# Gated stages of a hybrid model: the token's inverse root moved from the operand to the eviction, with the hand-over through a PSUM bank

## The chip, the cores and the metric

One core of one Trainium2 chip runs the whole program in one launch. The metric is the device time in microseconds, taken as the median of several runs. Everything is float32; each large product is made of three products of float32r halves.

## The reference, cut to what matters

A stack of two blocks on 256 tokens of width 1024. The first block has four layers (two RWKV-7 layers, a stick-breaking attention, a sparse attention), the second has two layers on two streams, `x` and `ctx`. Between the mixers stand eleven gated units (feed-forward), each fed by a root-mean-square norm; four take the plain norm, seven the modulated one:

```python
def rms_norm(x, g):
    xf = x.astype(jnp.float32)
    y = xf * lax.rsqrt(jnp.mean(xf * xf, axis=-1, keepdims=True) + RMS_EPS)
    return (y * g.astype(jnp.float32)).astype(x.dtype)

def swiglu(h, w_gu, w_down):
    g, u = jnp.split(h @ w_gu, 2, axis=-1)
    return (jax.nn.silu(g) * u) @ w_down
...
        x = x + swiglu(rms_norm(x, norm_ffn[i]), ffn_w_gu[i], ffn_w_down[i])
...
        x = x + 0.5 * mx[2] * swiglu_2(modulated_norm(x, norm_g[l, 0], mx[0], mx[1]), *ffn1)
```

`modulated_norm` is the same norm with a gain per channel and a shift per channel added after it. Width inside a unit: 2816.

## The kernel before, in words

Activations lie transposed in SBUF: 128 partitions hold channels, the free axis holds 8 chunks of 256 tokens (`X`, `CTX`). A projection is a list of weight panels, each 128x1024 (8 chunks deep, 128 output columns), planned in one fixed order (`order`). For each panel SyncE loads `raw` (4 slots), ScalarE makes the rounded half `whi` (L571), GpSimd the rest `wlo = raw - whi` (L561), and TensorE runs 24 matmuls (8 chunks by three products, L658), each of 256 columns, into one of four PSUM banks. ScalarE makes the `whi` of panel p+4 when panel p is done (semaphore `panels_done`), so it runs four panels ahead. VectorE empties the banks (`bank_free`).

A projection of 1024 outputs and depth 1024 has 8 steps of one panel. The down projection has 8 steps of three panels (8, 8 and 6 chunks). The up projection of a gated unit has 22 steps of two panels, gate and up; the two projections together have 1584 matmuls.

A gated unit (`act_ffn`, `pe_ffn`, `dve_ffn`) begins with the norm. ScalarE squares the 8 chunks into `W[8]` (L609; all but the last while the projection before still runs), TensorE sums them over partitions with a matrix of ones in 8 float32 matmuls (L738, each two records), ScalarE takes the square root (L724), VectorE the reciprocal `RSTD` (L744), then for each chunk VectorE multiplies by gain and `RSTD` (L760), ScalarE makes the rounded half `AH` (L731 with a shift, L733 without), VectorE the rest `AL` (L753 or L755). TensorE starts on a chunk when its `AL` is there. In the up loop ScalarE takes `silu` of the gate bank (L789), VectorE multiplies it with the up bank into bank 5 (L807) and splits the product into `HH` and `HL` (L809, L811).

Between the last gated unit of the first block (`ffn3`) and the first of the second (`f10x`) the context rows are turned (TensorE L1820, VectorE L1839) and `dve_ada` makes shifts and gains (L1911, L1915, L1921) and a scalar `LAM` (L1924, TensorE L1902, ScalarE L1898). `dve_ada` runs again between `f20x` and `f11x`. The eleven units follow these projections: four a mixer's output projection of the first block (`ffn0` to `ffn3`), three a mixer's output projection of the second (`f20c`, `f20x`, `f21x`), four a down projection (`f10x`, `f10c`, `f11x`, `f11c`).

## Time and profile before

| | |
|---|---|
| time, median of 3 runs | 4366.14 us (4362.85 to 4371.75) |
| profiled execution | 4345.92 us, span 4344.1 us |
| TensorE busy | 3865.0 us, 89% of the span |
| GpSimd busy | 2664.3 us, 61% |
| ScalarE busy | 1936.8 us, 45% |
| VectorE busy | 1603.7 us, 37% |
| granted TensorE clock, mean | 0.947 of full speed |

The profile is of one execution. Busy shares are averages over all stages: TensorE is the engine that most stages wait for, and what matters for a change is the stretch in which it waits.

### The profile page before, as it was taken

The page shows a single profiled execution, that of the slowest core. Times are in us where ns is not written, and L with a number is a line of the kernel's source. Part 1 is how long each engine was busy: PE and PEld are TensorE (multiplying, and loading weights), DVE is VectorE, ACT ScalarE, POOL GpSimd, SP SyncE. Part 2 cuts the span into 40 slices and gives each one's busy share as a digit, 9 for nine tenths or more (in the row PEclk, how much of TensorE's full clock was granted, in tenths as well). Part 3 has the DMA queues.
Part 4 walks back from the last instruction along what each step waited for, and adds up shares of the span by engine and source line. Part 5 has one row for each costly group of instructions (what it writes and reads, how often), then busy time and mean ns, then how long its engine had stood idle before and what let it go on. Part 6 is the DMA issues. An engine that isn't in the chain of part 4 may idle for free.

```text
span 4344.1 us, 94128 instructions
## 1 busy us (share of the span) xinstructions
PE 3865.0 (89%) x36305; PEld 3657.7 (84%) x36305; DVE 1603.7 (37%) x3002; ACT 1936.8 (45%) x2635; POOL 2664.3 (61%) x1186
## 2 busy tenths in 40 slices
PE   5897998999798989799999978998889999997799
PEld 5676997998498857798999868997789899996798
DVE  4544214214621454312121473227531212148421
ACT  3213446543353322444454464535544445446453
POOL 4103873786177400587877747875578687874676
PEclk8998999999799999899999999999899999999899
DMA  5453652564157445465665525654356565653455
GB/s 153 150 196 103 184 171 77 174 189 120 31 174 194 136 142 180 124 193 169 194 174 166 163 81 163 192 164 117 112 160 193 155 184 172 174 148 93 134 170 150
DMA packets 1177130, 664.74 MB, mean 153 GB/s; under 512 B 30141, under 2 KB 1138441, under 8 KB 1176743
## 3 DMA queue, kind: packets, MB, share of 16 engines
q1 hardware_dynamic: 1176871, 661.06, 51.7%
q8 instruction: 190, 3.11, 0.3%
q14 instruction: 69, 0.57, 0.0%
HBM read 659.92 MB, written 1.05 MB: 152 GB/s over the span
## 4 chain that ended last, share of the span: by engine, by line
PE 69%; issue 14%; POOL 7%; DVE 6%; ACT 2%; SPq 1%; DMA 1%; POOLq 0%; DVEq 0%; ACTq 0%
PE bank L658 56%; POOL wlo L561 7%; PE bank L738 2%; PE bank L637 2%; PE bank L991 1%; PE bank L821 1%; PE bank L1062 1%; PE bank L1085 1%; DVE RSTD L744 1%; PE bank L1091 1%; DVE W L760 1%; PE bank L894 1%; PE bank L1068 1%; PE bank L1093 1%; DVE AL L716 0%
## 5 line engine op out<-in xcount | busy, mean ns | idle before, releaser
L561 POOL TENSOR_TENSOR wlo<-raw,whi 128x1024 fp32r<-128x1024 f32 (+3 forms) x1182 | 2664.1, 2270 | 1656.0 <-ACT whi L571 1646.5
L658 PE MATMUL bank<-AH,whi 128*128 128x256 f32 x6320 | 1802.0, 285 | 192.0 <-DVE AL L716 104.5
L658 PE MATMUL bank<-AL,whi 128*128 128x256 f32 x6320 | 1784.1, 282 | 0.0
L658 PE MATMUL bank<-AH,wlo 128*128 128x256 f32 x6320 | 1782.1, 282 | 0.0
L571 ACT ACTIVATE whi<-raw 128x1024 fp32r<-128x1024 f32 (+3 forms) x1182 | 1173.2, 995 | 1159.0 <-PE bank L658 1006.2
L658 PEld LDWEIGHTS bank<-AH,whi 128*128 128x128 f32 x6320 | 1220.7, 193 | 209.9 <-issue 180.8
L658 PEld LDWEIGHTS bank<-AH,wlo 128*128 128x128 f32 x6320 | 1223.1, 194 | 0.0
L658 PEld LDWEIGHTS bank<-AL,whi 128*128 128x128 f32 x6320 | 1222.6, 193 | 0.1
L658 PE MATMUL bank<-HH,whi 128*128 128x256 f32 x1936 | 536.1, 277 | 0.0
L658 PE MATMUL bank<-HL,whi 128*128 128x256 f32 x1936 | 536.1, 277 | 0.0
L658 PE MATMUL bank<-HH,wlo 128*128 128x256 f32 x1936 | 536.1, 277 | 0.0
L807 DVE TENSOR_TENSOR bank<-silu,bank 128x256 f32<-128x256 f32 x242 | 103.9, 429 | 952.7 <-PE bank L658 952.7
L658 PEld LDWEIGHTS bank<-HH,wlo 128*128 128x128 f32 x1936 | 364.9, 188 | 0.0
L658 PEld LDWEIGHTS bank<-HL,whi 128*128 128x128 f32 x1936 | 363.4, 188 | 0.0
L658 PEld LDWEIGHTS bank<-HH,whi 128*128 128x128 f32 x1936 | 363.4, 188 | 0.0
L789 ACT ACT_TABLE_LOAD x101 | 129.6, 1283 | 175.0 <-PE bank L658 175.0
L789 ACT ACTIVATE silu<-bank 128x256 f32<-128x256 f32 x242 | 93.1, 385 | 248.4 <-PE bank L658 247.3
L704 DVE TENSOR_TENSOR X<-X,bank 128x256 f32 x64 | 27.0, 422 | 310.2 <-PE bank L658 310.2
L706 DVE SCALAR_TENSOR_TENSOR X<-bank,mod_x,X 128x256 f32 x48 | 23.2, 484 | 265.8 <-PE bank L658 265.8
L809 DVE CAST HH<-bank 128x256 f32 x242 | 102.9, 425 | 36.5 <-DVE bank L807 17.1
L658 PE MATMUL bank<-BRH,whi 128*128 128x256 f32 x240 | 77.6, 323 | 42.7 <-DVE BRL L716 18.2
L811 DVE TENSOR_TENSOR HL<-bank,HH 128x256 f32 x242 | 102.8, 425 | 31.3 <-DVE HH L809 2.9
(336 smaller groups left out, 4144.1 us busy)
## 6 DMA issues: line engine op xcount, KB each, us to landing
raw<-in_ffn_w SPq DMA_DIRECT2D x420, 512.0 KB, 3.8
raw<-in_w_in SPq DMA_DIRECT2D x182, 512.0 KB, 3.8
raw<-in_ffn_w_gu SPq DMA_DIRECT2D x176, 512.0 KB, 3.8
ada_raw<-in_w_ada SPq DMA_DIRECT2D x96, 512.0 KB, 6.0
raw<-in_ffn_w_down SPq DMA_DIRECT2D x64, 512.0 KB, 4.2
raw<-in_rw_w_rkv SPq DMA_DIRECT2D x48, 512.0 KB, 4.3
raw<-in_w_ada SPq DMA_DIRECT2D x48, 512.0 KB, 5.1
raw<-in_ffn_w SPq DMA_DIRECT2D x56, 384.0 KB, 3.5
```

The source lines that it names most:

```text
L561: pool.tensor_tensor(wlo[slot][:, 0:n], raw[slot][:, 0:n], whi[slot][:, 0:n], ALU.subtract).then_inc(lo_ready, 1)
L571: act.activation(whi[slot][:, 0:n], raw[slot][:, 0:n], ACT.Copy).then_inc(hi_ready, 1)
L637: mm = pe.matmul(ps, o, w, start=k == c == n == 0, stop=k == g.pps - 1 and c == nk - 1 and n == 2)
L658: mm = pe.matmul(ps[:, 0:o.shape[2]], w, o[:, k0 + c, :], start=tile not in started and c == n == 0, stop=last_panel and c == nk - 1 and n ...
L738: mm = pe.matmul(bank[4][:, 0:S], ones[:, :], W[8][:, c * S:(c + 1) * S], start=c == 0, stop=c == C - 1)
L744: dve.reciprocal(RSTD[:, :], STD[:, :]).then_inc(dve_step, 1)
L760: op = dve.scalar_tensor_tensor(h[:, o], x[:, o], gain(c), RSTD[:, :], ALU.mult, ALU.mult)
L789: act.activation(silu[j % 2][:, :], ps[:, 0:S], ACT.Silu).then_inc(silu_ready, 1)
L807: dve.tensor_tensor(hidden, silu[j % 2][:, :], banks[1][:, 0:S], ALU.mult).then_inc(bank_free, 2)
L809: dve.tensor_copy(HH[:, o], hidden).then_inc(dve_step, 1)
L811: dve.tensor_tensor(HL[:, o], hidden, HH[:, o], ALU.subtract).then_inc(hidden_ready, 1)
L821: mm = pe.matmul(bank[first + c // 2][:, (c % 2) * S:(c % 2 + 1) * S], mat, src[:, c * S:(c + 1) * S], start=True, stop=True)
```

## The change

The operand of a gated unit no longer carries the token's inverse root. ScalarE multiplies each finished chunk of the residual by the gain alone, into bank 5 (`SCALED`), squares the chunk into the other half of that bank (`SQUARE`), and makes `AH` by the same product; VectorE makes `AL` from the bank and adds the squares up. All this runs chunk by chunk inside the projection before (`SPLIT_AFTER`). TensorE sums two tiles of squares (`SQSUM`, `SQLAST`) after its first panel, and VectorE multiplies gate and up by `RSTD` when it empties the banks. Where the norm has a shift, the operand gets two more columns per chunk (the shift's rounded half and its rest), the matmuls on `AH` run over 258 columns, and the two extra columns of the result, summed, are the shift's share, added as a bias. So `AH` has a chunk every 320 columns, and the vector table `VEC` lies in the last 62 of them. The operands of the output projections go to `OUTH`, `OUTL` (`W[7]`, `W[8]`), since `A` is being filled for the unit behind.

```diff
+        AW = S + 64
-        AH, AL = sb("AH", C * S, F32R), sb("AL", C * S, F32R)
+        AH, AL = sb("AH", C * AW, F32R), sb("AL", C * S, F32R)
+        VEC = sb("VEC", C * AW, at=a_at)
...
+        A_SHIFTED = (AH_v[:, :, 0:S + 2], AL_v)
+        OUT = (v3(OUTH), v3(OUTL))
...
+        SPLIT_AFTER = {"rw0.out": "ffn0", "sb.out": "ffn1", "ds.out": "ffn2", "rw3.out": "ffn3", "ffn3.down": "f10x",
+                       "f10x.down": "f10c", "mix0c.o": "f20c", "mix0x.o": "f20x", "f20x.down": "f11x",
+                       "f11x.down": "f11c", "mix1x.o": "f21x"}
...
+                if split_for:
+                    if s > 0:
+                        act.wait_ge(bank_free, g.t0 + s)
+                    act_high_parts(act, split_for, chunks_until(FFN[split_for].after_own, s))
...
+        def act_high_parts(act, name, until):
+            f = FFN[name]
+            for c in range(high_made[0], until):
+                xc = f.x[:, c * S:(c + 1) * S]
+                if c == C - 1:
+                    act.wait_ge(partial_squares, after(act, partial_squares))
+                elif c:
+                    act.wait_ge(scaled_taken, after(act, scaled_taken))
+                act.activation(SCALED, xc, ACT.Copy, scale=f.gain(c))
+                if c < C - 1:
+                    act.activation(SQUARE, xc, ACT.Square)
+                act.activation(AH_v[:, c, 0:S], xc, ACT.Copy, scale=f.gain(c)).then_inc(hi_part, 1)
+                if c == C - 1:
+                    act.activation(SQLAST[:, :], xc, ACT.Square).then_inc(last_square, 1)
+            high_made[0] = max(high_made[0], until)
+
+        def dve_low_parts(dve, name, until):
+            for c in range(low_made[0], until):
+                dve.wait_ge(hi_part, after(dve, hi_part))
+                dve.tensor_tensor(AL_v[:, c, :], SCALED, AH_v[:, c, 0:S], ALU.subtract).then_inc(operand_ready, 1)
+                if c == 0:
+                    dve.tensor_copy(SQSUM[:, :], SQUARE).then_inc(scaled_taken, 1)
+                elif c < C - 1:
+                    done = scaled_taken if c < C - 2 else partial_squares
+                    dve.wait_ge(scaled_taken, after(dve, scaled_taken))
+                    dve.tensor_tensor(SQSUM[:, :], SQUARE, SQSUM[:, :], ALU.add).then_inc(done, 1)
...
         def act_ffn(act, name, x, shift=None):
-            act_norm(act, x, W[7], shift)
...
+                if k == 0 and isinstance(s, int) and s == 0:
+                    act.wait_ge(sums_ready, after(act, sums_ready))
+                    act.activation(STD[:, :], bank[4][:, 0:S], ACT.Sqrt, bias=eps[:, 0:1], scale=1.0 / D).then_inc(std_ready, 1)
+                if k == 1:
+                    act.wait_ge(gate_ready, after(act, gate_ready))
...
+                dve.tensor_tensor(bank[6][:, b * S:(b + 1) * S], banks[0][:, 0:S], RSTD[:, :], ALU.mult).then_inc(gate_ready, 1)
+                dve.wait_ge(panels_done, after(dve, panels_done))
+                if f.shift is not None:
+                    dve.tensor_reduce(offset[:, 2:3], banks[1][:, S:S + 2], AX_X, ALU.add)
+                dve.tensor_tensor(up, banks[1][:, 0:S], RSTD[:, :], ALU.mult).then_inc(bank_free, 2)
...
+        def dve_ffn_turning(dve, name, l, turn=None):
+            dve_ffn(dve, name)
+            dve_modulation(dve, l)
+            dve_lambda_in(dve, l)
+            between = {3: lambda: dve_lambda_out(dve, l)}
+            if turn:
+                between |= {0: lambda: turn(0), 1: lambda: turn(1)}
+            dve_residual(dve, f"{name}.down", FFN[name].x, FFN[name].out_gate, between)
```

`chunks_until` gives chunk s-1 at step s where the unit reads the stream that the projection is just updating (nine units), and chunk s where it reads the other stream (`f10c`, `f11c`). `dve_ffn_turning` serves `ffn3` and `f20x`: the context's turning and the making of shifts and gains move from behind the down projection into it.

On ScalarE, the end of the first RWKV layer's output projection and the head of `ffn0`, before (`W_92` is the squares' tile):

```order
L571 ACTIVATE whi_56<-raw_52 128x1024
L609 ACTIVATE W_92<-X 128x256 x2
L724 ACT_TABLE_LOAD
L724 ACTIVATE STD<-bank,eps 128x256
L733 ACTIVATE AH<-W_91 128x256 x8
L789 ACT_TABLE_LOAD
L789 ACTIVATE silu_81<-bank 128x256
```

and of the change at the same place:

```order
L583 ACTIVATE whi_56<-raw_52 128x1024
L642 ACTIVATE bank<-X,VEC 128x256
L644 ACTIVATE bank<-X 128x256
L645 ACTIVATE AH<-X,VEC 128x256
L642 ACTIVATE bank<-X,VEC 128x256
L645 ACTIVATE AH<-X,VEC 128x256
L647 ACTIVATE sq_98<-X 128x256
L583 ACTIVATE whi_53<-raw_49 128x1024
L886 ACT_TABLE_LOAD
L886 ACTIVATE STD<-bank,eps 128x256
L583 ACTIVATE whi_54<-raw_50 128x1024
L891 ACT_TABLE_LOAD
```

The square root and its table load now stand behind the first panel of the up projection, and what is left of the last two chunks stands ahead of it.

On VectorE, the stretch between `ffn3` and `f10x` before:

```order
L704 TENSOR_TENSOR X<-X,bank 128x256
L101 REGISTER_ALU
L101 COMPARE_AND_BRANCH
L1839 COPY CTX<-bank 128x512 x4
L1911 TENSOR_TENSOR mod_x<-both_115,VEC 128x72
L1915 SCALAR_TENSOR_TENSOR gain_x<-mod_x,VEC 128x8 x3
L1921 TENSOR_SCALAR mod_x<-mod_x 128x8 x2
L1911 TENSOR_TENSOR mod_c<-both_115,VEC 128x72
L1915 SCALAR_TENSOR_TENSOR gain_c<-mod_c,VEC 128x8 x3
L1921 TENSOR_SCALAR mod_c<-mod_c 128x8 x2
L1924 TENSOR_TENSOR LAM<-VEC_76 128x2
```

and with the change, where they stand behind the up loop of `ffn3` and ahead of its first residual:

```order
L2057 TENSOR_TENSOR mods<-both_119,VEC 128x72
L2061 SCALAR_TENSOR_TENSOR gains<-mods,VEC 128x8 x3
L2067 TENSOR_SCALAR mods<-mods 128x8 x2
L2057 TENSOR_TENSOR mods<-both_119,VEC 128x72
L2061 SCALAR_TENSOR_TENSOR gains<-mods,VEC 128x8 x3
L2067 TENSOR_SCALAR mods<-mods 128x8 x2
L2040 TENSOR_TENSOR LAM<-VEC_76 128x2
L791 TENSOR_TENSOR X<-X,bank 128x256
L669 CAST AH<-mods 128x8
L671 TENSOR_TENSOR AH<-mods,AH 128x8
L1971 COPY CTX<-bank 128x512 x2
L791 TENSOR_TENSOR X<-X,bank 128x256
```

Thirteen small operations, all from SBUF to SBUF, moved from a stretch between two projections to one in which panels are being prepared.

## Rows read from the trace of the kernel before

**Rows 1.** The page, part 1: busy time, share, instructions.

```profile
PE 3865.0 (89%) x36305; PEld 3657.7 (84%) x36305; DVE 1603.7 (37%) x3002; ACT 1936.8 (45%) x2635; POOL 2664.3 (61%) x1186
```

**Rows 2.** Waits of TensorE: total us, times, longest us.

```profile
PE bank L658 <- DVE AL L716: 104.5, 9, 18.8
PE bank L658 <- DVE AL L753: 49.1, 11, 5.6
...
PE bank L658 <- DVE AL L755: 25.3, 6, 4.5
```

**Rows 3.** The chain that ended last, whole span: start us, us, what.

```profile
774.59 3.47 PE bank L738 x16
782.21 181.68 PE bank L658 x1584
...
3396.89 189.74 PE bank L658 x1581
3586.62 3.47 PE bank L738 x16
3595.63 182.85 PE bank L658 x1584
```

**Rows 4.** The same chain, from 770 to 784 us.

```profile
778.09 0.48 ACT STD L724
...
778.66 1.76 DVE RSTD L744
```

**Rows 5.** The same chain, from 1968 to 1996 us.

```profile
1975.91 0.03 issue
...
1976.53 0.67 PE bank L1820 x4
...
1983.21 0.35 PE bank L1902 x2
...
1993.73 2.38 PE bank L658 x8
```

**Rows 6.** Windows of 4 us: busy by engine, then clock, DMA share, GB/s.

```profile
778.00:782.00 4.00, 0.05 (x1) 0.00 (x0) 3.30 (x6) 1.51 (x4) 0.12 (x1) 1.00 0.62 184
782.00:786.00 4.00, 3.79 (x17) 3.61 (x18) 4.00 (x13) 2.26 (x6) 0.00 (x0) 0.57 0.00 0
786.00:790.00 4.00, 4.00 (x37) 4.00 (x37) 0.39 (x2) 2.77 (x4) 0.11 (x1) 1.00 0.01 4
...
2888.00:2892.00 4.00, 2.19 (x19) 1.98 (x17) 0.42 (x1) 2.12 (x2) 2.09 (x1) 1.00 1.16 294
...
2388.00:2392.00 4.00, 2.49 (x12) 2.52 (x13) 0.09 (x1) 2.62 (x3) 4.00 (x3) 0.71 1.02 253
```

**Rows 7.** Windows of 100 us, line L658 alone: PE, PEld, clock, DMA.

```profile
440.00:540.00 100.00, 100.00 (x852) 100.00 (x851) 1.00 0.64 184
800.00:900.00 100.00, 100.00 (x885) 100.00 (x884) 1.00 0.66 192
```

**Rows 8.** Groups of instructions, shapes apart: busy us, mean ns, idle before.

```profile
L571 ACT ACTIVATE whi<-raw 128x1024 fp32r<-128x1024 f32 x998 | 1056.3, 1059 | 1011.1 <-PE bank L658 859.1 <-PE bank L637 53.6 <-DMA raw<-in_w_in 49.5
...
L789 ACT ACT_TABLE_LOAD x101 | 129.6, 1283 | 175.0 <-PE bank L658 175.0
...
L2323 DVE TENSOR_TENSOR W<-W,hid 128x256 f32 x48 | 42.9, 894 | 7.3 <-DVE hid L2321 3.7
...
L2321 DVE TENSOR_TENSOR hid<-silu,bank 128x256 f32<-128x256 f32 x72 | 30.4, 422 | 120.4 <-ACT silu L2207 116.0 <-DVE BRL L716 1.2 <-DVE W L2323 0.6
...
L731 ACT ACTIVATE AH<-W,mod_x 128x256 fp32r<-128x256 f32 x48 | 23.1, 505 | 22.9 <-DVE W L760 22.9
```

**Rows 9.** Timeline of GpSimd: an output projection, then an up projection.

```profile
758.81 2.40 POOL L561 TENSOR_TENSOR wlo<-raw,whi 128x1024 fp32r<-128x1024 f32 x1 [0.31 <-ACT whi L571]
...
844.29 9.50 POOL L561 TENSOR_TENSOR wlo<-raw,whi 128x1024 fp32r<-128x1024 f32 x4 [1.39 <-ACT whi L571]
```

**Rows 10.** Timeline of VectorE between `f20x` and `f11x`.

```profile
3381.71 2.62 DVE L1915 SCALAR_TENSOR_TENSOR gain_x<-mod_x,VEC 128x8 f32<-128x8 f32 x3
```

More of the change, by code:

```diff
@@ L270, in build @@
         HL = sb("HL", FC * S, F32R, at=w_at[0] + FC * S * 4)
+        OUTH = sb("OUTH", C * S, F32R, at=w_at[7])
+        OUTL = sb("OUTL", C * S, F32R, at=w_at[8])
+        SQSUM, SQLAST = (sb(f"sq{k}", S, at=w_at[5] + (C // 2 + k) * S * 4) for k in range(2))
         VF = sb("VF", C * S)
@@ L601, in act_panels, with chunks_until @@
                 per |= work.per
-            steps_of(act, g, per, step, last_straight=True)
+            if then:
+                per |= then.per
+            steps_of(act, g, per, step, peel=then is not None, last_straight=True)
         squared = [0]
+        high_made, low_made = [0], [0]
+        SCALED, SQUARE = bank[5][:, 0:S], bank[5][:, S:2 * S]
+        def chunks_until(own, s):
+            return s if own or s == 0 else s + 1
+        def act_high_parts(act, name, until):
[13 more added lines that the diff above has]
+            high_made[0] = max(high_made[0], until)
@@ new lines, in dve_shift_columns, with dve_residual @@
+        def dve_shift_columns(dve, name):
+            f = FFN[name]
+            if f.shift is None:
+                return
+            m = f.shift.unsqueeze(2)
+            dve.tensor_copy(AH_v[:, :, S:S + 1], m).then_inc(dve_step, 1)
+            dve.wait_ge(dve_step, after(dve, dve_step))
+            dve.tensor_tensor(AH_v[:, :, S + 1:S + 2], m, AH_v[:, :, S:S + 1], ALU.subtract)
+        def dve_residual(dve, name, x, gate=None, between=None):
+            g = G[name]
+            split_for = SPLIT_AFTER.get(name)
+            if not split_for:
+                dve_tiles(dve, name, take_residual(dve, x, gate))
+                return
+            tile = dve_tiles(dve, name, take_residual(dve, x, gate), by_hand=True)
+            own = FFN[split_for].after_own
+            for s in range(g.steps):
+                tile(s)
+                if s == 0:
+                    dve_shift_columns(dve, split_for)
+                dve_low_parts(dve, split_for, chunks_until(own, s))
+                if between and s in between:
+                    between[s]()
+            dve.wait_ge(bank_free, tiles_of(name))
@@ new lines, in pe_ffn, with norm_sums, pe_ffn_down @@
+        def pe_ffn(pe, name):
+            def norm_sums():
+                for k, (t, made) in enumerate(((SQSUM, partial_squares), (SQLAST, last_square))):
+                    pe.wait_ge(made, after(pe, made))
+                    mm = pe.matmul(bank[4][:, 0:S], ones[:, :], t[:, :], start=k == 0, stop=k == 1)
+                mm.then_inc(sums_ready, 1)
+            pe_panels(pe, f"{name}.up", chunked=True, after_first=norm_sums)
+        def pe_ffn_down(pe, name, by_hand=False):
+            return pe_panels(pe, f"{name}.down", chunked=True, chunk_ready=hidden_ready, by_hand=by_hand)
@@ L847, in build @@
         L_, VT, BT, CT = (W[7][:, k * Q4:(k + 1) * Q4] for k in range(4))
-        work = [sb(f"scan{k}", Q4, at=a_at + k * Q4 * 4) for k in range(7)]
+        work = [sb(f"scan{k}", Q4, at=l_at + k * Q4 * 4) for k in range(7)]
         IY, IX, IT, LOFF, RHS, SOL, STATE = (t[:, :] for t in work)
@@ L2464, in pe_second @@
         def pe_second(pe):
[L2465 to L2471 removed]
+            pe_ffn_all(pe, "f10x")
+            pe_ffn_all(pe, "f10c")
             pe_mix(pe, 0, "c")
[L2473 removed]
+            pe_ffn_all(pe, "f20c")
             pe_mix(pe, 0, "x")
[L2475 to L2478 removed]
+            pe_ffn_turning(pe, "f20x")
+            pe_ffn_all(pe, "f11x")
+            pe_ffn_all(pe, "f11c")
             pe_mix(pe, 1, "c")
             pe_mix(pe, 1, "x")
[L2481 removed]
+            pe_ffn_all(pe, "f21x")
             pe_norm(pe)
@@ L2517, in _ @@
                     sp_lora(sp, 1)
-                if g.name == "f10x.up":
+                if g.name == "ffn3.down":
                     sp_ctx(sp)
```

331 lines of the change are left out of this document (195 added, 136 removed).

## The prediction, made before the changed kernel ran

> **What bounds the kernel now.** I read the page first: TensorE is busy 3865 of 4344 us [rows 1], so a gain must come from its 479 idle us or from work taken off it. The list of its waits says where they are. Two entries belong to the norms whose multiplied chunks it waits for, 49.1 and 25.3 us [rows 2]; they include norms ahead of mixers, which stay. The largest, 104.5 us, is the split ahead of output projections and of the RWKV projections; it stays too. A wait alone does not price a norm, though, since TensorE sums squares in it. So I went to the chain. The sums of `ffn1` start at 774.59 and the up projection at 782.21, 7.6 us later; for `f11c` it is 9.0 [rows 3]. In between lie the eight sums (3.47), the root (0.48), the reciprocal (1.76) and the first multiplied chunks [rows 3, 4]. Nine of the eleven units have such a gap, between those two values, 71.9 us in sum. `f10x` also waits for the context's turning and for `dve_ada`: 1975.91 to 1993.73, 17.8 us [rows 5]. For `f11x` it is 15.2 us from the second kind of operation of `dve_ada`, at 3381.71, to the up projection at 3396.89 [rows 3, 10], and ahead of it lie the last residual and `dve_ada`'s first operation, which I put at 1.6: 16.8.
>
> A second cost lies behind the gap. In `ffn1`'s gap TensorE does nothing from 778 to 782; the clock is at 0.57 in the next 4 us and full again after (half is 1.2 GHz, full 2.4) [rows 6]. In a full window of an up loop 885 matmuls overlap 100 us, 882.5 without those that only hang over its left edge, so one takes 113.3 ns [rows 7]; 1584 of them make 179.5 us, and the chain has 181.7 for `ffn1` and 182.9 for `f11c` [rows 3]. So 2.2 to 3.4 us a unit go to the slow clock and to chunks that come slower than TensorE takes them, 31 us for eleven. What the change can touch is 71.9 + 17.8 + 16.8 + 31 = 138 us.
>
> **The same stream has two rates.** In `ffn0` 852 matmuls fall into 100 us, 117.7 ns each, at the same full clock [rows 7]. Two of the eleven units run so in this execution. Nothing waits in either, and I do not know what picks the rate. One unit at the slow rate costs 1584 x 4.4 ns = 7 us.
>
> **The change, part by part.**
>
> *At the restart, nine units.* Count from T, the end of the projection's last matmul. ScalarE owes one panel's `whi` (1.06 us), then chunk 6: a scaled copy, a square, `AH`. `AH` with a scalar from a table takes 0.505 [rows 8]; I take 0.5, 0.4 and 0.5, less what overlaps, 1.2 us: T+2.25. VectorE, with the residual behind it, makes `AL` and adds the square, 0.42 each, the price of its multiplication by a bank [rows 8]: T+3.1. Only then may ScalarE write chunk 7 into the bank, two operations, 0.9: T+4.05. `AL` is there at T+4.6. TensorE starts chunk 0 at T and would want chunk 7 after 21 matmuls, at T+2.2. Stall: 2.4 us. The two sums behind the first panel are a quarter of the eight, 0.87. Together 3.3, times nine: 29.7 us.
>
> *The other two* (`f10c`, `f11c`) have chunk 6 ready; chunk 7 follows at T+2.5, stall 0.3, with the sums 1.2 each: 2.4 us.
>
> *Turning and scalar.* TensorE keeps its 16 transposes, four of which take 0.67, and two `LAM` products, 0.35 each time [rows 5]: 3.4 us.
>
> *Clock.* A stall of 2.4 us, in two pieces around a chunk, is shorter than the 8 us that cost the clock. Short stalls go both ways: TensorE was busy 2.19 of 4 us around 2890 and the clock stayed at 1.00, 2.49 of 4 us around 2390 and it was 0.71 [rows 6]. I take one in three of the nine to cost what half the clock costs in 3.4 us, 1.7: 5 us. Bounds: 0 and 15.
>
> [...]
>
> *Root, reciprocal, table loads* leave the path: the first up eviction ends some 10.5 us after T (first panel with its stall 5.0, `whi` 1.06, load 1.28, root 0.48, reciprocal 1.76, two multiplications [rows 4, 8]). TensorE needs those banks back for the third step, 14.2 us after T (four panels of 2.72, stall and sums). The cover is about 4 us. Each us beyond it costs 1 us in each of eleven units.
>
> *The up loop.* VectorE goes from three operations a step to five of 0.42 and, with a shift, two tiny ones: 2.6 us of a 5.4 us step. ScalarE's work per step is the same. Neither gets near TensorE. In an output projection ScalarE now has 1.06 + 1.2 of 2.72 us a panel. Cover if wrong: four slots, of which the panel itself needs 1.06 + 2.4 us.
>
> *GpSimd* is the engine with no room: 2.40 us a panel in an output projection, four in 9.50 of 10.9 us in an up loop [rows 9]. Does more work on VectorE slow it or get slowed by it? VectorE's multiplication of SBUF by a bank takes 422 ns, and its sum of two SBUF tiles of the same shape, in the same loop, 894 on average [rows 8]. Three operations of 8 columns took 2.62 us together while a panel was made [rows 10]. So two SBUF operands wait for GpSimd to finish and one bank operand does not. All new operations of the loop and of `AL` read a bank. They cost what they cost alone.
>
> The Trainium skill has this as a rule: the two engines share a port pair that is locked for a whole instruction, when VectorE reads two SBUF tensors or copies in its two-port mode (SBUF — State Buffer, "SBUF: two separate sides"). The trace agrees, 894 against 422.
>
> *Thirteen small SBUF operations* move into that traffic, at the end of `ffn3` and `f20x`, and two more (the shift's columns) with each shift. Each may wait up to 2.40 us: 31 us if each meets a panel, some 3 us if none. After a panel GpSimd is idle 0.3 us, room for one or two; I take 15 us from T+4. The first residual of the down projection, due 7.5 us after its start, then comes at 19. ScalarE waits for that residual at step 1, from 16 on; TensorE has four panels in hand. In `f20x` that is covered. In `ffn3` TensorE itself waits behind step 1 (at 15.9) for VectorE's copies of the first half of the context, which come at 20 to 23: 4 to 7 us. With 31 us instead, ScalarE would be held, panels would stop, GpSimd fall idle and VectorE be free, so the loss ends near 10 a unit. I take 6 for both; bounds 0 and 20.
>
> *258 columns.* 7 units x 22 steps x 2 panels x 8 chunks x 2 products = 4928 matmuls have two more columns. No row shows that width. From below: a matmul takes 113.3 ns where 256 columns at 2.4 GHz need 106.7, so something else paces it and two columns may be free. From above within the stream: 2/2.4 = 0.83 ns each, 4 us. Far end: a second pass of the stream, 107 ns each. I take 1 us, as the row at 113.3 leaves 6.6 ns.
>
> [...]
>
> *At nothing:* chunks 320 apart (the split's copies keep rows of 256 adjacent columns), `OUTH`/`OUTL`, the moved scan tiles, the tables. The split into the strided `AH` stands on the path ahead of the RWKV projections; if it went at half its pace it would cost about 1.2 us six times, 7.
>
> **Sum.** After: 29.7 + 2.4 + 3.4 + 5 + 6 + 1 = 47.5 us against 138. Saved 90.5. The profiled execution, 4345.92 (its span and 1.8 around it), would be 4255. The median of the runs is 20 us above that execution; two slow-rate units of eleven in the profile leave room for more of them in the runs. I carry the difference over: 4366 - 91 = 4275.
>
> **The rivals.**
>
> 1. *As above*: nearly all gaps go. 4275, own range 4250 to 4295. Chance 0.65.
> 2. *A new wait takes over part.* The late chunk 7, VectorE's blocked operations or the thin cover of the first eviction cost 3 to 8 us more in most units. For: the last two chunks go through one bank and back and forth twice. Against: each step is priced from a row. 4300 to 4345; 0.15, of which 0.03 lies within 0.2% of no change and 0.01 above.
> 3. *The rate.* With fewer restarts whole runs of units share one rate. If nine more units ran at 117.7 it would be 63 us back: 4338; half of it 4307. For: the rate holds through both projections of a unit. Against: most restarts in the profile chose 113.3. Chance 0.10. The opposite, fewer slow ones than the timed runs had and no clock loss, gives 4230 to 4245: 0.06.
> 4. *Slower: the 258 columns fall off the fast path.* Place: the `AH` products of the seven shifted units. It decides from 90.5 us / 4928 = 18 ns each; with a second pass of 107 it is 527 - 91 = 436 more, 4802. For: no row has this width. Against: all that the trace shows is proportional to columns. Chance 0.04.
>
> **How the numbers follow.** Faster by over 0.2% (9 us, about what can be told from no change): 0.65 + 0.11 + 0.10 + 0.06 = 0.92. Same 0.03. Slower 0.01 + 0.04 = 0.05. The range takes all of case 1, half of each neighbour below and above it and most of the lower part of case 2: 4245 to 4312.
>
> **What would show it.** The sums should be two matmuls behind the first panel; the distance between the last matmul of a projection and the first of the unit should be under 0.5 us, and chunk 7 should come 4.6 us after T. `AL` from a bank should take 0.42. TensorE's wait in `ffn3`'s down projection should be 4 to 7 us. Matmuls on `AH` in `f10x` should keep 885 in 100 us. I am wrong if the first eviction comes later than 14 us after the unit began, if GpSimd's panel grows beyond 2.5 us in the up loop, or if 100 us of a shifted unit hold fewer than 850.

## The result, and the profile after

The changed kernel takes 4289.61 us (median of 4 runs, 4284.73 to 4293.22) beside 4364.50 for the kernel before on the same chip (4 runs, 4353.61 to 4371.75): a ratio of 0.983, 95% interval 0.9806 to 0.9854. That is 75 us faster. The forecast was 4275, its range 4245 to 4312.

The page of the changed kernel, part 1, has 132 matmuls fewer, and TensorE busy for 14 us less, not more [rows 1]:

```profile
PE 3850.9 (90%) x36173; PEld 3647.9 (85%) x36173; DVE 1846.4 (43%) x3797; ACT 1865.4 (43%) x2633; POOL 2673.1 (62%) x1186
```

The waits of TensorE (total us, times, longest us). L804 is now the split ahead of output and RWKV projections, L841 and L843 the low parts of the norms that stayed, L654 the new low part out of the bank:

```profile
PE bank L743 <- DVE OUTL L804: 73.6, 7, 18.8
PE bank L743 <- DVE AL L804: 30.2, 2, 15.3
...
PE bank L743 <- DVE AL L841: 18.2, 4, 5.6
...
PE bank L743 <- DVE AL L654: 16.7, 18, 1.3
...
PE bank L743 <- DVE AL L843: 8.3, 2, 4.2
```

The two norm entries of [rows 2], 49.1 and 25.3 us, have become 18.2 and 8.3 (the norms that stayed) and 16.7 (new). Now one restart, `ffn1`, as the chain of the work that ended last shows it (start us, us, what). The projection ends at T = 767.64:

```profile
763.89 3.75 PE bank L743 x33
767.64 0.02 issue
767.66 0.28 ACT whi L583
767.95 0.69 issue
768.63 0.46 ACT bank L642
769.09 0.31 ACT bank L644
769.40 0.44 ACT AH L645
769.84 0.02 issue
769.86 0.42 DVE AL L654
770.29 0.34 DVE sq L660
...
770.72 0.10 ACT bank L642
...
771.13 0.50 ACT AH L645
...
771.72 0.44 DVE AL L654
772.16 0.04 issue
772.20 0.86 PE bank L743 x3
773.06 1.71 PE bank L903 x4
```

TensorE starts the unit at once, but it gets its chunk 7 only 4.56 us after T: chunk 6 is made first, behind a cast of a weight panel, and chunk 7 waits for the square at 770.29. The two float32 sums of squares (L903, four records) follow behind the three products of chunk 7, here at a low clock (0.57 granted between 772 and 776). The gap of 7.6 us [rows 3] has become a stall of some 2 us inside the stream.

Then the stream itself. Windows of 100 us, line L743 alone: us, then TensorE and its weight loads with their counts, clock, DMA share, GB/s. The first is `ffn0`, the second `ffn1`, the third `ffn3`, the last three `f10x`, `f10c` and `f11x`:

```profile
440.00:540.00 100.00, 100.00 (x851) 100.00 (x850) 1.00 0.64 186
800.00:900.00 100.00, 100.00 (x885) 100.00 (x884) 1.00 0.65 190
1800.00:1900.00 100.00, 100.00 (x884) 100.00 (x884) 1.00 0.69 203
2000.00:2100.00 100.00, 100.00 (x845) 100.00 (x844) 1.00 0.62 182
2190.00:2290.00 100.00, 100.00 (x847) 100.00 (x846) 1.00 0.62 181
3380.00:3480.00 100.00, 100.00 (x844) 100.00 (x843) 1.00 0.63 184
```

In every unit with a shift some 40 matmuls are missing from 100 us, at full clock and with no wait. Taking off the 2.5 that only hang over an edge, as before, one matmul takes 118.7 ns there in place of 113.3 [rows 7] (the mean distance from start to start, read from the trace, is 118.9). It isn't the wide ones alone: the distances from start to start between 2000 and 2090 us are, on the mean, 118.0 behind the first 258-column product, 120.4 behind the 256-column one on `AL`, 118.3 behind the second wide one.

Lengths of the seven up projections with a shift, first matmul to first matmul of the down projection, in us, read from the traces (`e1_narrow` and `e10`, the kernel with a steady run of wide products, are experiments below):

```
               f10x   f10c   f20c   f20x   f11x   f11c   f21x    sum
before        122.1  122.7  123.1  122.1  128.1  122.8  123.5  864.4
changed       130.3  126.6  128.8  128.8  128.8  126.6  128.8  898.7
e1_narrow     124.7  125.4  123.0  127.6  124.7  125.4  123.0  873.8
e10           126.4  126.4  126.4  126.4  126.4  126.4  126.4  884.8
```

All stretches together, profile against profile: ahead of the units 95.8 us less, up projections 40.7 more, down projections 2.4 more, 52.7 us in sum (spans 4344.1 and 4291.4).

### The profile page after: what moved, and what is told of

Read it like the earlier page. It is cut to its first block, busy times and chain, and to the rows that moved or that the text cites. A ratio compares the mean times of both kernels' runs of the same rounds, so it can differ in the third digit from the quotient of the medians.

```text
span 4291.4 us, 94696 instructions
## 1 busy us (share of the span) xinstructions
PE 3850.9 (90%) x36173; PEld 3647.9 (85%) x36173; DVE 1846.4 (43%) x3797; ACT 1865.4 (43%) x2633; POOL 2673.1 (62%) x1186
## 4 chain that ended last, share of the span: by engine, by line
PE 68%; issue 15%; POOL 8%; DVE 6%; ACT 2%; SPq 1%; DMA 1%; POOLq 0%; DVEq 0%; ACTq 0%
PE bank L743 56%; POOL wlo L573 8%; PE bank L722 2%; PE bank L1123 1%; PE bank L1194 1%; PE bank L953 1%; PE bank L1217 1%; PE bank L1223 1%; PE bank L826 1%; PE bank L1026 1%; PE bank L1200 1%; PE bank L1225 1%; DVE W L848 0%; DVE RSTD L832 0%; DMA raw<-in_rw_w_rkv 0%
## 5 line engine op out<-in xcount | busy, mean ns | idle before, releaser
L743 PE MATMUL bank<-AH,whi 128*128 128x256 f32 (+1 forms) x5872 | 1665.7, 284 | 85.4 <-DVE AL L804 30.2
L743 PE MATMUL bank<-AL,whi 128*128 128x256 f32 x5872 | 1659.8, 283 | 0.0
L743 PE MATMUL bank<-AH,wlo 128*128 128x256 f32 (+1 forms) x5872 | 1654.3, 282 | 0.0
L743 PEld LDWEIGHTS bank<-AH,whi 128*128 128x128 f32 x5872 | 1128.1, 192 | 98.7 <-issue 51.6
L743 PEld LDWEIGHTS bank<-AL,whi 128*128 128x128 f32 x5872 | 1121.7, 191 | 0.6
L743 PEld LDWEIGHTS bank<-AH,wlo 128*128 128x128 f32 x5872 | 1121.7, 191 | 0.0
L743 PE MATMUL bank<-HH,whi 128*128 128x256 f32 x1936 | 536.4, 277 | 0.0
L743 PE MATMUL bank<-HH,wlo 128*128 128x256 f32 x1936 | 536.0, 277 | 0.0
L743 PE MATMUL bank<-HL,whi 128*128 128x256 f32 x1936 | 536.0, 277 | 0.0
L743 PEld LDWEIGHTS bank<-HH,whi 128*128 128x128 f32 x1936 | 364.6, 188 | 0.0
L743 PEld LDWEIGHTS bank<-HH,wlo 128*128 128x128 f32 x1936 | 363.6, 188 | 0.0
L743 PEld LDWEIGHTS bank<-HL,whi 128*128 128x128 f32 x1936 | 363.4, 188 | 0.0
L743 PE MATMUL bank<-OUTH,whi 128*128 128x256 f32 x448 | 132.0, 295 | 73.6 <-DVE OUTL L804 73.6
L932 DVE TENSOR_TENSOR bank<-bank,RSTD 128x256 f32<-128x256 f32 x242 | 103.2, 426 | 159.6 <-PE bank L743 159.5
L743 PEld LDWEIGHTS bank<-OUTH,whi 128*128 128x128 f32 x448 | 91.3, 204 | 75.7 <-issue 75.7
L743 PE MATMUL bank<-OUTL,whi 128*128 128x256 f32 x448 | 130.5, 291 | 0.0
L743 PE MATMUL bank<-OUTH,wlo 128*128 128x256 f32 x448 | 130.3, 291 | 0.0
```

The source lines that it names most:

```text
L743: mm = pe.matmul(ps[:, 0:o.shape[2]], w, o[:, k0 + c, :], start=tile not in started and c == n == 0, stop=last_panel and c == nk - 1 and n ...
L932: dve.tensor_tensor(up, banks[1][:, 0:S], RSTD[:, :], ALU.mult).then_inc(bank_free, 2)
```

## The experiments

The kernel before was timed again beside each set of runs: 4369.81 us beside `e1` to `e4`, 4360.23 beside `e5` to `e8`, 4355.78 beside `e9` to `e12`, 4364.50 beside the changed kernel. Kernels of different sets are therefore compared by their ratio to it (in brackets) and by their traces, and a few us between their medians show nothing.

**The width.** The seven shifted units get narrow operands; nothing is left to reduce, so the two reduces of a step become memsets, and the shift is left out.

```diff
-        A_SHIFTED = (AH_v[:, :, 0:S + 2], AL_v)
+        A_SHIFTED = (AH_v[:, :, 0:S], AL_v)
-                    dve.tensor_reduce(offset[:, b:b + 1], banks[0][:, S:S + 2], AX_X, ALU.add)
+                    dve.memset(offset[:, b:b + 1], 0.0)
```

> The products of the seven shifted units are 256 columns wide again, and the two reduces of each step are replaced by memsets of the offset to nought; so this kernel leaves out the modulation's shift, and all else is the changed kernel. Theory A, the width: the two extra columns cost 5.7 ns on each of 7392 matmuls (mean start to start 119 ns against 113.3 in the units without a shift), so the seven up projections return to 113.3 ns, some 885 matmuls in 100 us in place of 845, and the time falls by 7392 x 5.7 ns = 42 us, from 4289.6 to about 4248. Theory B, the layout or the traffic: the operand's chunks 320 columns apart, or ScalarE and VectorE at the banks, slow these matmuls; then they stay at 119 ns and the time stays within 5 us of 4289.6.

Measured: 4273.75 us (ratio 0.98, 0.9766 to 0.9833), by the medians 16 us under the changed kernel and not 42. Windows in `f10x` and in `f10c`:

```profile
1990.00:2090.00 100.00, 100.00 (x885) 100.00 (x884) 1.00 0.65 192
...
2160.00:2260.00 100.00, 100.00 (x852) 100.00 (x851) 1.00 0.63 184
```

Four of the seven units run at 113.3 ns, three (`f10c`, `f20x`, `f11c`) at 117.7, and these three keep 117.8 through their down projections, 2.4 us more each. The theory named the right cause and the wrong price: narrow units take part in the choice between two rates that `ffn0` already showed before the change [rows 7]; the wide ones never get the quick one. The up projections of these seven are 24.9 us shorter, the down projections of the three 7 us longer; 18 net, against 16 of the medians. The reduces went with the width here, but they aren't the cause: in the last two kernels with wide products below, 16 short runs of 258-column products that nobody reduces went at 118.0 to 120.4 ns on the mean.

**One wide product of three.**

```diff
+                            o = o[:, k0 + c, 0:S if w is wl else o.shape[2]]
-                            mm = pe.matmul(ps[:, 0:o.shape[2]], w, o[:, k0 + c, :], start=...
+                            mm = pe.matmul(ps[:, 0:o.shape[1]], w, o, start=...
```

> Of the three products of a chunk only the first (high weights by high operand) is 258 columns wide; the product of the low weights is 256 wide, so the kernel leaves out the low weights' part of the shift. Reduces and layout are the changed kernel's. If each wide matmul carries its own cost (8.5 ns, two in three wide now), the mean falls from 119 to about 116.2 ns and the time by 21 us to about 4269. If it is enough for the rate that wide and narrow matmuls alternate, it stays at 119 ns and 4290. If the reduces or the layout were the cause, it stays there too.

Measured: 4290.51 us (0.9839, 0.9801 to 0.9877). A window in `f10c`:

```profile
2160.00:2260.00 100.00, 100.00 (x852) 100.00 (x851) 1.00 0.63 184
```

That is exactly the slow rate, 117.7, in all seven units; so there is no price per wide product: one in three is enough to hold the slow rate, and the second adds 1.0 ns on the mean. It came with something not expected: the down projections behind all seven units began at 117.8, and six of them kept it (62.2 us in place of 59.8; that of `f20x` went to 113 behind the float32 product for `LAM`), where the changed kernel has 113.3 seven times.

**More columns, off and on a coarser grid.** First 264 columns with chunks 328 apart, then 272 with chunks 336 apart.

```diff
-        AW = S + 64
+        AW = S + 72          # second kernel: S + 80
-        A_SHIFTED = (AH_v[:, :, 0:S + 2], AL_v)
+        A_SHIFTED = (AH_v[:, :, 0:264], AL_v)          # second: 0:272
```

> The two high-operand products are 264 columns wide in place of 258 (chunks 328 columns apart; the six columns more hold copies of the shift and are not read behind). If a column past 256 costs what the two extra ones seem to cost (8.5 ns a wide matmul, 4.3 ns a column), a wide matmul takes 34 ns more than a narrow one, the mean is about 136 ns and the time about 4290 + 7392 x 17 ns = 4415. If there is one step at 256 and columns cost what they cost elsewhere (113.3 ns for 256, 0.44 ns each), six columns cost 2.7 ns on two in three matmuls, 13 us: about 4303.

> The two high-operand products are 272 columns wide and the operand's chunks 336 columns apart: both are multiples of 64 bytes, as 264 columns and chunks 328 apart were not (those put every product that reads the operand, narrow ones too, at a mean of 119.4 ns). Theory A, the grid: what lies on such a grid runs at the quick rate and the columns cost 0.44 ns each, so the shifted units come to 113.3 + 2/3 x 16 x 0.44 = 118.0 ns a matmul, those without a shift back to 113.3 or 117.8, and the time to about 4280. Theory B, any difference of widths between neighbours holds a stretch at the slow rate: 117.8 + 4.7 or more, 122.5 to 124 ns, and a time of about 4315 to 4325.

Measured: 4331.32 us (0.9914, 0.9888 to 0.994) and 4342.38 us (0.9963, 0.9947 to 0.998). Windows of 264 columns, in `ffn0` (256-column products, chunks 328 apart) and in `f10c`:

```profile
450.00:550.00 100.00, 100.00 (x843) 100.00 (x842) 1.00 0.63 184
...
2200.00:2300.00 100.00, 100.00 (x828) 100.00 (x828) 1.00 0.61 179
```

and of 272 columns, in `ffn1` (256-column products, chunks 336 apart) and in `f10c`:

```profile
800.00:900.00 100.00, 100.00 (x852) 100.00 (x851) 1.00 0.63 185
...
2200.00:2300.00 100.00, 100.00 (x819) 100.00 (x819) 1.00 0.61 179
```

Columns beyond 258 are cheap: 118.7, 121.1 and 122.5 ns for 258, 264 and 272, 0.27 to 0.4 ns of the mean for each column more. So it is a step between 256 and 258, theory B of the second kernel. (No kernel here has all three products wide, so whether the width or the change of width from one product to the next holds the slow rate isn't separated.) Both times lie above what the step and the columns give, since a second cost came in: with chunks 328 or 336 apart no up projection ran at 113.3, not even with 256 columns (119.0 and 117.7 ns; the distances rise at the first matmul on `AH`, ahead of any wait), while the down projections, whose chunks are 256 apart, began at 113.3 eleven times of eleven in both. With chunks 256 or 320 apart both rates occur. 1024 and 1280 bytes are multiples of 256 bytes, 1312 and 1344 are not; two strides on each side are few for a rule, but my rule in the expectation, 64 bytes, falls with 1344.

**Can single wide products set the rate?**

```diff
+                if marked and not first_step and n == S and (o is A[0] or o is OUT[0] or o is HID[0]):
+                    t = AH if o is A[0] else OUTH if o is OUT[0] else HH
+                    at = c * (AW if o is A[0] else S)
+                    return ps[:, 0:S + 2], w, t[:, at:at + S + 2]
```

> The runs so far show two rates of 256-column matmuls, 113.3 and 117.8 ns, and that a stretch keeps its rate: behind a unit whose last product is 258 (or 264) columns wide, the projection down ran at 113.3 in 18 of 18 cases; behind one whose last product is narrow it kept 117.8. In this kernel the first and one late product of each step of every projection without a shift are 258 columns wide too (the two more columns are not read). Theory A: a wide product brings a slow stretch back to the quick rate within a few matmuls, so nearly all stretches without a shift show a median of 113 ns (of 256-column ones at full clock less than 10% slow, against 47% in the changed kernel), and the time falls by 5 to 20 us, to about 4278, the more the more of a run was slow. Theory B: a wide product among quick ones as often throws them onto the slow rate; then most of these stretches show 118 and the time rises by 20 to 60 us.

Measured: 4318.59 us (0.9903, 0.9875 to 0.9932), by the medians 29 us more than the changed kernel: theory B. Behind their start three of the four up projections without a shift run at 117.5 ns on the mean and `ffn0` at 115.3. Most down projections take 61.1 us, between the 59.8 of the quick and the 62.2 of the slow rate: stretches of 113 and of 118 take turns in them. A single wide product among narrow ones turns the rate both ways.

**The scan's tiles in their new place, all else as before.**

```diff
-        work = [sb(f"scan{k}", Q4, at=a_at + k * Q4 * 4) for k in range(7)]
+        work = [sb(f"scan{k}", Q4, at=l_at + k * Q4 * 4) for k in range(7)]
```

> The kernel before with one part of the change alone: the scan's scratch tiles lie where the low-rank weights were, not in the operand's place. The changed kernel's two RWKV mixers came out some 8 to 10 us longer than the nine gaps' sum allows. If the place of these tiles costs that, the two stretches ahead of ffn0 and ffn3 (421.3 and 402.7 us before) are 4 us longer each and the time is some 8 us above the kernel before, 4374. If it is only chance in when the clock falls during the chain of the scan, the median stays within 5 us of the kernel before, and these two stretches scatter about 421 and 403.

Measured: 4354.81 us beside 4360.23 (0.9991, 0.9967 to 1.0014): no cost. The stretches ahead of `ffn0` and `ffn3` took 425.0 and 406.0 us, 3.7 and 3.3 more than in the first profile, and a second profile of the changed kernel had 415.4 and 397.3 where the first had 416.8 and 403.2. These stretches scatter by 4 to 6 us from one execution to the next; the gain that seemed to be missing there is within that.

**The hand-over through SBUF in place of the bank.**

```diff
-        SCALED, SQUARE = bank[5][:, 0:S], bank[5][:, S:2 * S]
+        SCALED, SQUARE = (sb(n, S, at=w_at[5] + (C // 2 + 2 + k) * S * 4)[:, :] ...
```

> The changed kernel with SCALED and SQUARE in SBUF in place of the bank, so that VectorE's subtraction for the low part and its sum of squares have both operands in SBUF. Theory A: such an operation can't run beside GpSimd's subtraction of a panel (2.40 us), as four of the moved modulation operations showed in ffn3 (2.35 us for one of some 0.05); at each restart the low part of chunk 6 or its square then waits for the end of GpSimd's panel, chunk 7 comes 1 to 2.4 us later, TensorE's waits on the low parts grow from 16.7 us to 26 to 38, the clock falls at more restarts, and the time rises by 12 to 35 us, to about 4310. Theory B: the bank matters little, since the chain is ScalarE's; then the waits stay within 3 us and the time within 5 us of 4290.

Measured: 4350.24 us (0.9967, 0.9942 to 0.9993), by the medians 61 us more than the changed kernel: theory A, and dearer than its upper end. The low part, one line of the trace (duration min/median/max), and TensorE's wait for it:

```profile
L654 DVE TENSOR_TENSOR AL<-scaled,AH x88: 424/1520/2496, 405.8 to 4146.6; 128x256 fp32r<-128x256 f32 x88
...
PE bank L743 <- DVE AL L654: 54.6, 27, 3.4
```

The same operation out of the bank, in the changed kernel:

```profile
L654 DVE TENSOR_TENSOR AL<-bank,AH x88: 416/425/426, 402.9 to 4089.9; 128x256 fp32r<-128x256 f32 x88
```

The waits explain 38 of the 61 us. Behind them the clock is low: the sums of nine of the eleven units ran at half the clock (1.35 us from the first to the next panel in place of 0.67), in the changed kernel those of three; at some 1.6 us a unit (`ffn1` took 124.7 us, `ffn3` 123.0, both at 113.3 ns) the six more make about 10 us. The bank is no detail of the change: without it four fifths of the gain are gone.

**The modulation twice.**

```diff
             dve_modulation(dve, l)
+            if l == 0:
+                dve_modulation(dve, l)
```

> The modulation of the first layer is computed twice in ffn3 (the second time gives the same numbers): 12 operations more on VectorE, 8.3 us by the trace of the changed kernel, ahead of VectorE's first tile of the projection down. Theory A: what hides the modulation is the 9.3 us until TensorE asks for the transposed half of CTX (it waited 0.25 us there, from 1917.8), so the cover is used up and all of the addition shows: TensorE waits 8 to 9 us at the second group of transposes, and the time rises by 8 to 12 us (the clock falls behind such a wait), to about 4300. Theory B, four banks deep: VectorE may be a tile or two late at no price, the wait stays under 2 us and the time within 3 us of 4290.

Measured: 4309.34 us (0.9889, 0.9857 to 0.9921), 12.5 above the control below. TensorE's waits for the context's first half, first in the changed kernel, then here:

```profile
PE bank L1952 <- DVE CTX L1971: 0.2, 1, 0.2
```

```profile
PE bank L1952 <- DVE CTX L1971: 6.5, 1, 6.5
```

Theory A: the down projection of `ffn3` grew by 6.6 us in the profile. The wait was forecast at 8 to 9 us; of the 8.6 us that VectorE spends more, 2.1 came back at the cast L669, which took 0.17 us here and had waited for a panel in the changed kernel (2.30). The change put the modulation into a place that hides all of it but a quarter of a us, and nothing is left to spare there.

**A shorter restart.** The high parts of a chunk are made in the step of its own tile, the last chunk's ahead of the next cast and through bank 7, without the wait for the squares.

```diff
-            return s if own or s == 0 else s + 1
+            return s + 1 if own or s else 0
...
+                    if early and k == g.pps - 1:
+                        act.wait_ge(bank_free, g.t0 + s + 1)
+                        act_high_parts(act, split_for, C)
...
-                if c == C - 1:
-                    act.wait_ge(partial_squares, after(act, partial_squares))
-                elif c:
+                if c and c < C - 1:
                     act.wait_ge(scaled_taken, after(act, scaled_taken))
-                act.activation(SCALED, xc, ...
+                act.activation(SCALED if c < C - 1 else SCALED_LAST, xc, ...
```

> The high parts of a chunk are made in the same step as its tile, the last chunk's ahead of ScalarE's next cast and through a bank of its own, without the wait for the partial sum of squares. If the 2.4 us that TensorE waits for the last chunk at nine restarts is this chain (one chunk's work queued behind another's and the cast), chunk 7 is there before TensorE asks, the waits on the low parts fall from 16.7 us to under 3, the slow clock behind some restarts goes too, and the time falls by 17 to 27 us, to about 4268. Rival: the cast made 1.1 us later starves GpSimd's subtraction, whose panel takes 2.4 us, and TensorE waits for panels 2 or 3 later; then what is gained at chunk 7 is given back, and the time stays within 6 us of 4290.

Measured: 4279.73 us (0.9795, 0.9766 to 0.9823), by the medians 10 us less than the changed kernel, where 17 to 27 were forecast. The restart of `ffn1` (timeline of ScalarE and VectorE; the projection ends at 772.4):

```profile
773.04 0.48 ACT L644 ACTIVATE bank<-X,VEC 128x256 f32<-128x256 f32 x1 [1.21 <-DVE X L793]
773.46 0.49 ACT L647 ACTIVATE AH<-X,VEC 128x256 fp32r<-128x256 f32 x1
...
773.98 0.42 DVE L656 TENSOR_TENSOR AL<-bank,AH 128x256 fp32r<-128x256 f32 x1 [1.04 <-ACT AH L647]
774.16 1.04 ACT L583 ACTIVATE whi<-raw 128x1024 fp32r<-128x1024 f32 x1
```

Chunk 7 is there 2.0 us after the end, TensorE waits for no low part at all (16.7 us before), and no later wait took its place. The mechanism is as expected, and the shifted units show its price, since their rate is the same in both kernels: the seven take 884.9 us in place of 898.6, 2.4 us less in a unit like `f20c`, 13.7 in sum. The time fell by less than forecast because the units without a shift gave their part back to the slow rate: `ffn0`, `ffn1` and `ffn3` went up at 117.8 here, the first two down as well (in the changed kernel `ffn0` alone), so the four up projections are 3.9 us shorter in sum.

**A steady run of wide products.** On top of the shorter restart, wide products in the last step of the first block's output projections and plain up projections.

```diff
+                if burst and isinstance(s, int) and s == g.steps - 1 and k == g.pps - 1 and cc < nk - 1 and n != 1:
+                    t, at = (AH, c * AW) if o is A[0] else (OUTH, c * S)
+                    return ps[:, 0:S + 2], w, t[:, at:at + S + 2]
```

> The kernel with the shorter restart (no wait on the last chunk, 4279.7 us) and one thing more: in the last step of the four mixers' output projections of the first half and of the four up projections without a shift, the high-operand products of seven chunks are 258 columns wide, with a narrow chunk behind them. Theory A: a steady run of alternating widths always ends in the quick rate when narrow ones follow (18 of 18 so far, where single wide products among narrow ones only tipped it to and fro); then ffn0 to ffn3 up and ffn0 to ffn2 down run at 113.3 ns, where the shorter restart alone had 117.8 in five of these seven, and the time falls by 10 to 20 us to about 4265. Theory B: the rate behind such a run is as open as elsewhere; then it stays at 4280 within 6 us, with some of these stretches at 117.8.

Measured: 4268.81 us (0.9797, 0.9763 to 0.9832; 28 us under the control below, in the same set of runs), the lowest median here. But the shorter restart alone had 0.9795 in its set, so no gain over it is shown: the fall of 11 us between the two medians is no more than that of the kernel before, 14, between the two sets. The traces say why. The first half of theory A holds, a steady run leaves the quick rate, and the three down projections run at 113.3; but all four up projections run at 117.8, `ffn2` too, which had the quick rate in the shorter restart. All up and down projections together take 2045.2 us, in the shorter restart 2045.8. The distances from matmul to matmul (ns) in `ffn1`, at the end of the run of wide products and the beginning of the unit (first line), and around the sums of squares one panel later (second):

```
119 120 115 118 122 119 113 113 114 113 113 114 113 113 114
113 114 113 113 117 | sums, four records: 215 215 215 28 | 305 118 117 119 117 118 118 118
```

The run of wide products does end in 113. The two float32 products with the matrix of ones end it. At full clock, between narrow products and with no stall ahead of them that happened in 11 of 11 cases (four here, four in the next kernel, three in the shorter restart), and the one unit that came to the sums at 118 (`ffn2` in the shorter restart) left them at 113. The sums turn one rate into the other. Where a stall stands just ahead of them, either rate followed: in the changed kernel, at full clock, 118 in `ffn0` and 113 in `ffn3`. Other float32 products turn the rate too: the first eight transposes of the context in `ffn3`'s down projection did it in all nine traces whose projection came to them at 113 (the changed kernel's two included), and in the changed kernel the rest of that projection stayed at 118: 2 us of the 4.5 by which it is longer than before.

**One wide product, put last.**

```diff
+                        products = (...) if oh.shape[2] == S else ((wh, oh), (wh, ol), (wl, oh[:, :, 0:S]))
+                        if oh.shape[2] > S and k0 + c > 0:
+                            products = products[::-1]
```

> The kernel of the run before it, and in the shifted units only the product of the high weights by the high operand 258 columns wide, put last of the three (first in a tile's first chunk); the low weights' part of the shift is left out. With one wide product first of three, these units ran at 118.8 ns against 119.9, and the projections down behind them at 117.8 in place of 113.3. Theory A: the order decides only what comes behind: these units keep some 118.8 (8 us less than with two wide) and, ending wide, hand on the quick rate, so the time is some 8 us below that of the run before it, about 4258. Theory B: the last tile's rate doesn't depend on which product ended it; then the seven projections down run at 117.8 (2.4 us each) and the time is 8 us above it.

Measured: 4274.82 us (0.9816, 0.978 to 0.9853), 6 above the kernel of the run before it. The ranges of the two overlap; the traces decide for theory B: the shifted units shrank from 126.4 to 125.5 us, the seven down projections went from 59.8 to 62.2. What hands on the quick rate is not that a wide product comes last but the run with two of them around a narrow one: it did so behind every shifted unit of the six kernels that have it with 258 columns and no single wide ones, 42 of 42.

**The changed kernel again.**

> The changed kernel as it is, for a second profile of it on the chip of these runs. If the two RWKV stretches are chance, ahead of ffn0 and ffn3 scatter by some us about 417 and 403 us; the time should be 4290 within 5 us, the seven shifted units at 119.8 ns again and the projections down behind them at 113.3, as these follow from the layout and not from chance; ffn0's rate may be either.

Measured: 4296.79 us (4290.22 to 4303.99; 0.9859, 0.9824 to 0.9893), 7 above the first median. The up projections of `ffn0` and `ffn2` ran at 117.8, those of `ffn1` and `ffn3` at 113.3, the shifted ones behind their start at 118.9 on the mean as in the first profile, the down projections behind them at 113.3.

## Why the prediction was right, and where it was not

The direction and the mechanism of the gain held, and the time lies within the range, in part by luck, since one term was far too small. Step by step:

- *The gaps.* As forecast, the distance from projection to unit is nothing in all eleven.
- *The restart.* T+4.6 forecast, T+4.56 measured, in the order named. The stall was put at 2.4 us; TensorE's waits sum to 16.7 over nine units, 1.9 each, and a shifted unit with the stall loses 2.4 by it (128.8 us against 126.4). That the chain is ScalarE's queue and the one bank, e4_restart shows by taking both away. The first eviction began 10.7 us after T and ended at 11.2 (forecast 10.5); the cover of 4 us held.
- *The clock* was low behind three of eleven restarts (forecast: three of nine), at 1.6 us each, about 5.
- *The up loop.* GpSimd's panel stayed at 2.40 us, the operations that read a bank at 0.42. The step behind this, that two SBUF operands wait for GpSimd and one bank operand does not, is shown by e8_sbuf: median 1.52 against 0.42. It is the rule of the Trainium skill that the prediction cited (SBUF — State Buffer, "SBUF: two separate sides"), and both traces agree.
- *The moved modulation was over-priced.* The step said 15 us taken, from T+4, and a wait of 4 to 7 us for the context, 6 us in the sum. The timeline of VectorE in `ffn3`:

```profile
1904.88 0.49 DVE L2057 TENSOR_TENSOR mods<-both,VEC 128x72 f32<-128x72 f32 x1 [0.28 <-DVE HL L944]
1905.41 2.77 DVE L2061 SCALAR_TENSOR_TENSOR gains<-mods,VEC 128x8 f32<-128x8 f32 x3
1908.21 1.91 DVE L2067 TENSOR_SCALAR mods<-mods 128x8 f32<-128x8 f32 x2
1910.15 0.29 DVE L2057 TENSOR_TENSOR mods<-both,VEC 128x72 f32<-128x72 f32 x1
1910.47 2.68 DVE L2061 SCALAR_TENSOR_TENSOR gains<-mods,VEC 128x8 f32<-128x8 f32 x3
...
1913.79 0.42 DVE L791 TENSOR_TENSOR X<-X,bank 128x256 f32<-128x256 f32 x1
1914.13 2.30 DVE L669 CAST AH<-mods 128x8 fp32r<-128x8 f32 x1
```

  Thirteen operations took 8.9 us, since only three of them met a panel (2.35, 1.70 and 2.26 us) and the rest fit between two; the wait was 0.25 us. The mechanism is right, and e9_mod_twice shows that the cover ends just there.

- *The 258 columns: the term that failed.* The step said "I take 1 us, as the row at 113.3 leaves 6.6 ns", with bounds of 0 and 4 within the stream. It treated the rest beyond 106.7 ns as free room. Two of three products with two extra columns hold the whole stream, the 256-column product on `AL` too, at the slow rate and 1 ns more: 7392 matmuls at 118.7 in place of 113.3 are 40 us where they would have been quick, 8 where slow anyway; the up projections of e1_narrow are 24.9 us shorter. The step also counted only the 4928 wide ones. The prediction's own sign of being wrong (under 850 in 100 us of a shifted unit) came true: 845. The Trainium skill (TensorE: Matmul & The Clock Gate, "Back-to-back issue gap") gives columns/2.4 + 2.5 ns at full clock, 110 for 258 columns, but calls it the gap of an isolated matmul and says that in a stream with weight loads both set the spacing. The trace is 8.7 ns above the formula here.
- *Rival 3, the rate.* "I do not know what picks it" was the honest half; the other half was to see that this rival and the width are one question. Its price per unit, 7 us, was right.
- *The sum.* 91 us were forecast against the profiled execution and 53 came, a miss of 38. By stretches: the up projections were to grow by 7 us (29.7 + 2.4 + 5 + 1 less the 31 of before) and grew by 40.7, the term above for the most part. Ahead of the units 106.5 us (71.9 + 17.8 + 16.8) were to go and 95.8 went; most of that miss lies ahead of `ffn0` and `ffn3`, within the scatter of e7_scan_moved. The down projections were to grow by 9.4 (3.4 + 6) and grew by 2.4. The medians differ by 75, because the 20 us between profile and median of before, which I carried over, are not there after: the runs of before lie between 4336.8 and 4382.8, those of the changed kernel between 4284.7 and 4304.0. A likely reason, not tested, is that seven of its units no longer take part in the choice of the rate. So the forecast is within 15 us partly because two errors have opposite signs, and that is luck.

**What stays open:** what makes the two rates. What sets them here is known in part: the sums turn one into the other, a steady wide/narrow/wide run leaves the quick one, 258 columns in one or two of three products exclude it, and so do strides of 1312 or 1344 bytes. A kernel with the steady run behind the sums, in place of before them, should bring `ffn0` to `ffn3` to 113.3 and, by my estimate, save 4.4 us each (125.1 us for `ffn0`, 120.7 for `ffn2` in the shorter restart); it wasn't run.

## What to carry to other kernels

That a stream's mean distance is above columns over clock doesn't mean that it has room to give away: count 100 us windows before and after any change of an operand's width, stride or neighbours, because a change of 1% in the columns moved all its matmuls here by 5%. Where a handed-over value is read by VectorE while GpSimd works, hand it over in a bank (0.42 us an operation against 1.52). A stall that a move leaves behind is read from the queue of the engine that feeds it: here a cast and one shared buffer ahead of the last chunk, worth 2.4 us a unit once the order was turned. Work that is hidden with nothing to spare is a wait in the next version. And compare a small step with a kernel of the same set of runs: between sets the same kernel moved by up to 14 us.

## What the hardware showed that I had not expected

- 256-column float32r matmuls run at 113.3 or 117.8 ns at the same full clock, and the rate lasts through whole units until something turns it.
- Two float32 products with a matrix of ones turned it in 12 of 12 cases between narrow products at full clock with no stall ahead of them; behind a stall either rate followed.
- 258 columns: 118.7 ns on the mean of three products of which two are wide; with one wide, 117.7; with 264 and 272 columns 121.1 and 122.5.
- With chunks 1312 or 1344 bytes apart no stretch of 256-column reads had the quick rate (119.0 and 117.7 ns); with 1024 and 1280 both rates occur.
